# A new order of pieces in a two-block transformer kernel, with its weight splits written into it

## The chip, the cores and the metric

One core of a Trainium2 chip runs the whole program. The metric is the device time of one execution in microseconds. The kernel before took 2286.56 us (median of three runs, 2283.53 to 2306.3).

## The reference

Activations are 256 tokens of 1024 features in float32. The first block has two layers, each of: SwiGLU (width 2816), a mixer, cross attention onto 256 memory tokens, SwiGLU. The mixer of layer 0 is differential attention beside stick-breaking attention; that of layer 1 is latent attention (MLA, 16 heads). The second block has two layers, each of three mixers on one projection, an output projection with layer norm, and a SwiGLU with layer norm:

```python
o_gla = _gla_mixer(...)        # gated linear attention, 4 heads
o_rwkv = _rwkv7_mixer(...)     # delta-rule recurrence, 4 heads
o_nsa = _nsa_mixer(...)        # 8 heads: compressed, selected, window attention
mix = jnp.concatenate([o_gla, o_rwkv, o_nsa], axis=-1) @ w_out[l]
x = _layer_norm(DEEPNORM_ALPHA * x + mix, ln1_w[l], ln1_b[l])
```

NSA's output is `gt[0]*o_cmp + gt[1]*o_slc + gt[2]*o_win` per head. With 256 tokens, the selection takes in every block, so the kernel computes the second and third parts as two causal attentions with keys and values of their own.

## The kernel before

**Stages.** Twelve stages run in the order f0, m0, c0, f1, f2, m1, c1, f3, b0, f4, b1, f5: `f` is a SwiGLU, `m0` and `m1` are the mixers of the first block, `c0` and `c1` its cross attentions, `b0` and `b1` the three mixers of the second block with output projection and layer norm. The activation `x` stays in SBUF as eight slices of 128 features by 256 tokens.

**Weights.** Every weight is read once, in units of up to 128x1024 values, by SyncE's queue into a ring of 6 buffers (`RING`). A float32 product is made of three reduced-precision ones, so each unit is split: ScalarE writes the rounded part (`w_hi`), VectorE the rest (`w_lo`), and TensorE multiplies hi by hi, hi by lo and lo by hi. There are 4 pairs of buffers for split units (`NU`). A split has to wait for its load and for TensorE to have used the unit that held the pair before. `act_splits` and `dve_splits` (lines 376 and 391) are called after every piece; each splits all units that the next piece needs, and further ones if a test (`can_split`) on the orders allows it.

**Pieces and orders.** A stage is a list of pieces, such as "the second half of the query projection" or "step 1 of attention unit 5". All five engines walk through the same list, and each does its own share of a piece, in order; semaphores keep them together where data pass. So a piece is short on one engine and long on another, and a piece in the wrong place makes an engine stand in front of a wait while later work is ready. In the `f` stages the list is written by loops. In the six others it is a string (`WEAVE`, line 40): every letter names a chain, and takes that chain's next piece (`woven`, line 1204). In `c0`, `p` is the query chain (projection half, sum of squares, projection half, norm, turns), `a` to `d` are four attention units of three steps (scores, turn, values), and `o` is the output projection and the eight updates of `x`. In `b0` and `b1`, `r` is the delta rule's main chain and `s` its second inner part, `g` and `h` gated linear attention, `l` and `n` the projections and the compressed part of NSA, `u` `v` `w` `a` `b` five lanes of its 16 attention units, and `m` the output projection and the layer norm.

**Fillers.** The letter `z` is a "warm" piece: TensorE alone does something there, the product of two identity matrices into a PSUM bank that is known to be idle (`pe_warm`, line 3092). One such float32 product is recorded as two matmuls of 128 columns. Where no bank is known to be idle, nothing is issued.

**Update of x.** `act_x`, `dve_x` and `pool_x` (lines 644 to 668) prepare the next stage's input for each slice: ScalarE rounds it, VectorE computes the rest, GpSimd adds up squares. A root mean square (`rs`) needs all eight squares; TensorE sums them over partitions.

**GLA.** Scores within a chunk are summed over seven levels (`ge`). Each level takes differences on GpSimd, exponentials on ScalarE, two multiplies on VectorE, eight matmuls into two banks, and a masked multiply of each bank on VectorE; from level 1 on GpSimd adds the two results onto the matrix `P` (lines 2783 to 2870).

**NSA.** Compressed attention writes `mix`; each of 16 attention units then adds its gated output onto `mix` (line 2202 on). The five lanes' score buffers lie over buffers of the compressed part.

## Time and profile before

| | |
|---|---|
| runs | 2283.53, 2286.56, 2306.3 us |
| span of the profiled execution | 2285.3 us (no other time of it is listed) |
| TensorE matmul busy | 2202.2 us, 96% |
| VectorE, ScalarE, GpSimd busy | 1526.7, 1104.3, 418.3 us (67%, 48%, 18%) |
| weight splits on VectorE | 571 instructions, 694.2 us |
| DMA | 310.32 MB, mean 136 GB/s |

A busy TensorE only says that matmuls were running, fillers too. "PEclk" is the granted clock of TensorE as a share of 2.4 GHz. L140 is the line of the one helper that issues all matmuls, L165, L171, L177, L182 and L192 those of VectorE's and GpSimd's operations, L154 and L191 those of ScalarE's; tiles have to be told by their names (`ps` PSUM, `consts` the identity, `ring`, `w_hi`, `w_lo` weights, `scratch` the stage buffers, `rows` the squares).

### The profile page before, as it was taken

Reading aid. Unit: us, or ns where it says so; the run is one execution under the profiler, and the core shown is the slowest. Engines: PE = TensorE matmul, PEld = TensorE weight load, DVE = VectorE, ACT = ScalarE, POOL = GpSimd, SP = SyncE. Lnnn points to the kernel's source line nnn. Section 1 sums busy time; section 2 is a strip of 40 time slices with the busy share of each in tenths; the row PEclk is TensorE's granted clock in tenths of the full one; section 3 lists DMA queues with packets and bytes.
Section 4 is the critical chain, followed back from the end, with each engine's and each line's share of the span. In section 5 each row is a group of like instructions: output and inputs, shape, how many; then the busy total and the mean of one; then the engine's idle time right before and its main releaser. Section 6 shows DMA issues by size and latency. Waiting matters only on the chain.

```text
span 2285.3 us, 36711 instructions
## 1 busy us (share of the span) xinstructions
PE 2202.2 (96%) x14388; PEld 1953.8 (85%) x14388; DVE 1526.7 (67%) x2709; ACT 1104.3 (48%) x1997; POOL 418.3 (18%) x379
## 2 busy tenths in 40 slices
PE   6999999999999999999999998999998999999997
PEld 5888888988888888999888987889887988788886
DVE  5976765587678667756876685456766586456765
ACT  4654454365456544535654522346555432345554
POOL 2521001122112100012220030101213123101223
PEclk9999999999999999999999999999999999999999
DMA  6545432254555443133544321114544320303552
GB/s 242 192 170 173 148 130 74 74 192 182 180 194 190 177 157 133 38 111 130 188 179 174 139 85 61 57 38 152 186 181 149 133 94 1 116 29 127 187 178 90
DMA packets 88444, 310.32 MB, mean 136 GB/s; under 512 B 9808, under 2 KB 11600, under 8 KB 87760
## 3 DMA queue, kind: packets, MB, share of 16 engines
q1 hardware_dynamic: 87984, 305.29, 37.5%
q8 instruction: 114, 1.87, 0.3%
q10 hardware_dynamic: 288, 2.69, 0.3%
q14 instruction: 58, 0.48, 0.1%
HBM read 306.89 MB, written 1.05 MB: 135 GB/s over the span
## 4 chain that ended last, share of the span: by engine, by line
PE 91%; DVE 4%; ACT 2%; DMA 1%; issue 1%; POOL 0%; SPq 0%; DVEq 0%; ACTq 0%; POOLq 0%
PE ps L140 89%; PE ps L145 2%; DVE scratch L165 2%; DMA ring<-in_w 1%; ACT w_hi L154 1%; DVE w_lo L165 1%; ACT scratch L154 0%; DVE x L165 0%; DVE scratch L192 0%; DVE stats L182 0%; POOL scratch L165 0%; ACT scratch L191 0%; DVE scratch L177 0%; DVE scratch L171 0%; SPq L207 0%
## 5 line engine op out<-in xcount | busy, mean ns | idle before, releaser
L165 DVE TENSOR_TENSOR w_lo<-ring,w_hi 128x1024 fp32r<-128x1024 f32 (+2 forms) x571 | 694.2, 1230 | 420.0 <-ACT w_hi L154 414.3
L140 PE MATMUL ps<-h,w_hi 128*128 128x512 f32 (+1 forms) x2784 | 872.2, 372 | 24.0 <-DVE h L177 19.1
L154 ACT ACTIVATE w_hi<-ring 128x1024 fp32r<-128x1024 f32 (+2 forms) x571 | 581.5, 1032 | 487.0 <-PE ps L140 485.4
L140 PE MATMUL ps<-h,w_lo 128*128 128x256 f32 x2448 | 688.0, 281 | 0.0
L140 PEld LDWEIGHTS ps<-h,w_hi 128*128 128x128 f32 x2784 | 504.2, 190 | 123.3 <-issue 21.4
L140 PEld LDWEIGHTS ps<-h,w_lo 128*128 128x128 f32 x2448 | 465.0, 190 | 0.0
L140 PE MATMUL ps<-f,w_hi 128*128 128x512 f32 (+1 forms) x1444 | 419.2, 356 | 3.2 <-DVE f L165 3.2
L140 PE MATMUL ps<-f,w_lo 128*128 128x256 f32 x1184 | 331.9, 280 | 0.0
L165 POOL TENSOR_TENSOR f<-f_work,f 128x256 fp32r<-128x256 f32 x132 | 187.7, 1422 | 596.2 <-ACT f L154 596.1
L140 PEld LDWEIGHTS ps<-f,w_hi 128*128 128x128 f32 x1444 | 254.4, 189 | 46.1 <-DVE w_lo L165 3.6
L140 PE MATMUL ps<-scratch 128*128 128x128 f32 (+9 forms) x1952 | 256.3, 300 | 8.7 <-DVE scratch L192 2.5
L140 PE MATMUL ps<-consts 128*128 128x128 f32 x1912 | 246.5, 280 | 0.0
L140 PEld LDWEIGHTS ps<-consts 128*128 128x128 f32 x1912 | 233.5, 195 | 10.3 <-issue 6.1
L140 PEld LDWEIGHTS ps<-scratch 128*128 128x128 f32 (+4 forms) x1952 | 210.4, 186 | 33.0 <-issue 10.7
L140 PEld LDWEIGHTS ps<-f,w_lo 128*128 128x128 f32 x1184 | 223.9, 189 | 0.1
L191 ACT ACTIVATE scratch<-ps 128x512 f32<-128x512 f32 (+9 forms) x203 | 98.5, 499 | 221.7 <-PE ps L140 171.8
L140 PE MATMUL ps<-w_hi,h 128*128 128x512 f32 (+2 forms) x528 | 161.2, 380 | 0.1
L165 POOL TENSOR_TENSOR rows<-x 128x256 f32<-128x256 f32 x64 | 40.7, 636 | 589.5 <-DVE x L165 583.1
L165 DVE TENSOR_TENSOR f_work<-f_work,ps 128x256 f32<-128x256 f32 x306 | 126.6, 415 | 3.6 <-ACT f_work L191 3.5
L165 POOL TENSOR_TENSOR scratch<-scratch 128x512 f32<-128x512 f32 (+1 forms) x69 | 87.9, 1276 | 201.1 <-DVE scratch L165 83.6
L165 DVE TENSOR_TENSOR f_work<-f_work 128x256 f32<-128x256 f32 x264 | 113.8, 431 | 8.6
L140 PEld LDWEIGHTS ps<-w_hi,h 128*128 128x128 f32 x528 | 98.8, 190 | 15.9 <-issue 1.2
(136 smaller groups left out, 2136.4 us busy)
## 6 DMA issues: line engine op xcount, KB each, us to landing
ring<-in_w SPq DMA_DIRECT2D x520, 512.0 KB, 3.3
ring<-in_w SPq DMA_DIRECT2D x48, 384.0 KB, 3.4
ring<-in_w SPq DMA_DIRECT2D x16, 396.0 KB, 4.8
stage_consts<-in_ctwo ACTq DMA_DIRECT2D x1, 1344.0 KB, 5.9
stage_consts<-in_cthree ACTq DMA_DIRECT2D x1, 1281.0 KB, 6.8
stage_consts<-in_cone SPq DMA_DIRECT2D x1, 1083.0 KB, 5.7
x<-in_x SPq DMA_DIRECT2D x4, 256.0 KB, 4.4
scratch<-in_m SPq DMA_DIRECT2D x1, 1024.0 KB, 6.7
```

The costliest lines, as they stand in the source:

```text
L140: return self.e.matmul(out, lhsT, rhs, start=start, stop=stop, skip_group_check=free)
L145: return self.e.transpose(out, x, self.K.ident[0:x.shape[0], 0:x.shape[0]])
L154: return self.e.activation(out, x, func, **k)
L165: return self.e.tensor_tensor(out, a, b, op)
L191: return self.e.activation(out, a, ACT.Copy)
```

## The change

- **Strings.** All six `WEAVE` strings are new. Fillers go from 1009 to 287 marks (b0 282 to 55, b1 284 to 71, c0 95 to 36, c1 86 to 36, m0 80 to 24, m1 182 to 65). Two new marks place weight splits: `.` is the next unit's split on ScalarE, `,` on VectorE (131 and 146 of them). In stages with such marks the automatic calls only split what the next piece needs; in the `f` stages they are as before. The other letters come as often as before, but for `b` (gone in the blocks), `u` to `a` and `m`.
- **`dve_x`** does the update of slice j before the rest of slice j-1 and not behind it.
- **GLA.** From level 1 on, VectorE copies each bank straight into `P` where the level's mask is set (`copy_predicated`), and GpSimd adds nothing. Some waits name other steps in turn.
- **NSA.** Attention units write into an accumulator of their own (`ao`); a new piece `nA`, once for each half of the tokens, adds it to `mix` on VectorE. There are 4 lanes for 5, the buffers lie elsewhere, and the keys are rotated in the order 1, 2, 0, 3.
- **Latent attention.** The two latent vectors get buffers of their own in place of those of the stage's input, and queries, outputs and the fifth lane move. TensorE turns the output in pieces of the new layout.

The strings with their marks, and the core of the rest:

```diff
@@ -37,27 +37,23 @@
 NORMED = ("f0", "m0", "c0", "f1", "f2", "m1", "c1", "f3")
+MARKS = {"z": "warm", ".": "split_hi", ",": "split_lo"}
 WEAVE = {
-    "b0": ("zzzzzzzzzrzzrrrrrgzgzgrhlzhzhzzzzrzzzhzzzzzzzrzzhrzzzhzgzzhzzzzzzzhzzzzzzzzhzzhzzzzzzzzzzrzzzzzz"
-           "zzzzhhrhzzzzzzzhzzzzzzlzhzzzzhzrrrzzhzrlhzhzzrrzszzzhzrzsrzzzhzzzsszhzzzzzszzszzzzznzzzzzzzzzzrz"
-           "rzzzzzzzzsrnznzrzzzzzzrznzzzzzzzznnnzzzzzzzzzznzzwzzzzzzzzzzzzzzzzzzzzzrzzzzzzzzzzzzzzzzvrsvrrnz"
-           "zzzzzzrzzrnrnzrzzzzzzzzzzzrwzzrurnrsunsuwvsrsbsusrvrrruzvbrvrarvrwbabuwurwaawrauramurzvzwbuabzbv"
-           "awzzbumabummzmzzzmmmmmmmzmmmmzzzzzzzzzzzmmzzmzmmmmmmzmzmzmzzmzzzzzzzzmzzzmzzzzzmmmmzzzz"),
-    "b1": ("zzzzzzzzzzrzrrgrzgrgrhgzzrrlhzzzzzzzzzzzzzzzzzzzzzhhzzzrzzzrzzhhzzhzzzzzzzzzzzzzzzzzzzzzzzzzzzzz"
-           "zzzzzzzzzzzzzrhhhzzrzzhzzhzzzzzzlzzzrzzrzzzzzzzzzzzrrhhzrshzzhzsrzzlsszhrhszzrhzrrhrzhsrhzzzzzzz"
-           "zzszrzzzzszrzzznrzszzzzzznzrsnrzzznzznzzzzzznrrrnwzzzzzzzzzzzzzzzzzzzzzzznzzzzzzzzzzruzzzzzzzzzz"
-           "zzzzzzzzzzzzzzzzzrsrwnzrznzszzszzrsrzzrrnzrrnrnrzurvrwwbuavrrvmrvzzrvzzzzazbubvwbauawwuaubwvauab"
-           "buvuwvazbuambummmzzzzmzmmmmmmzmzzzzmmmzmmmmmmmmzzzzmzzzmzzzzzmzmzzmzmzzzzmzzzzmzmzzzzmzzm"),
-    "c0": ("zzzzzzzzzpppzzzzpzzzzzzzzzzzzzzzzzzzzzzzzzzzzzzzzzzzzzzzzzzzpzpazcbacdbzacdbdozozzzozoozoozzozoo"
-           "zzzzzzozozzzzzzzzzzzozzzzzzzzz"),
-    "c1": ("zzzzzpppzzzpzzzzzzzzzzzzzzzzzzzzzzzzzzzzzzzzzzzzzzzzzzppazbdazbcdabcdcozzoozozozzooozozzzoozzzzz"
-           "zzzzzzzzzzzzzzzoozzzz"),
-    "m0": ("zzypzzzzzqqzzzzzqzzzzzzzzkzkqzzpzzzzzzzzzzzzzzzzkyzzzzzzykbakyqlycvaycvbaabcacbcaacctbsbatscaacc"
-           "tassactszczssotzystzztssyzzzootsttotstoozzozzzzzzzzozzoozozoozoozzzzzozoozzzzzz"),
-    "m1": ("zyzpzzzzzqqzqzkkqzyzqyzzkzqqzqkzzzqkzzzzzzzzzzzzzzzzzzzzzzzzzzzzzzzzkzzzzzzzzzzzzzzzzzzzzzzzzzzz"
-           "zzzzzzzzzzzzzkzzzzzzhzzzzzzzzzzzzzzzzzyzzzzzzzyzttzzttzzzzyztzzzzzzzzzttztzzzzzzzzzzzzzuzuzyuayu"
-           "zuucauducbadacbedacbedbacaebcodaceabcbedadebecdzaobedaeoozozzzozoozoooooozozzzzozozzzzzzzzzzzzzz"
-           "z"),
+    "b0": ("r,.,.r..,,r,,..r,.r.r,zzzzzzzzzrrrrhg,.,.gzzrrgzzzhh.h.zzzzzrrzh,,rrrhh,.gh,,hs,.hhsl,h.,s,.hh,h"
+           "rzzlrrh.hr.rhhrhs,s,,h.,rhlrszrnzzzrszzzznnrzzzrnzzzzznzzzzznzznwsuvarruwswruaruaavwsrvursruwsaw"
+           "ravwausrruwvnsrvvurwravzznranr.w.rvurnur.wvaru,mvrnrnma,wvam.m,mmmmzzzzm,.mmmmmm..,,..,mmmmmmmmm"
+           "mmmzzzzmmmmmmmmmm"),
+    "b1": ("zzzzzzzzzzzzzzzzzzr,.,.r,,..r.,.,r.,r.zzhr.g,,.r,r.g,.rrg.,,.,.,zzzhhhg..r,h,rlhhzrrrrh,,h,r,hrh"
+           "zzzzlhr,,h,sh,hszzlrhrrshhrshsrhrhsrhzzzrsnzzzzsrzzzzzzzzznnzzzzzzzzzznrnzzznzzznruvsruwsuawrsra"
+           "uwvwarawvrsurvrwsarvrnaswauurrvrwuaznrwn.ruu.ravrawunrm,varvnrwvr.n,.mwvu,avmm,mm.mmzzzzm,mmmm,m"
+           ",mm,mm....mmmmmmmmmzzzzmmmmmmmmmm"),
+    "c0": (".pppp..zzzzzzzzzzzzzzzzzzzzzzzzzzzzzzzzp,pzbcabdcabdc.ad.ozo,zzooo.,oo.o,oo.o,o,,o"),
+    "c1": ("pp.,ppzzzzzzzzzzzzzzzzzzzzzzzzzzzzzzzzp..pzbadbc,adbcadc.ozozzo,oo.,o,.o,ooo.,.o,oo"),
+    "m0": ("q..p,,q.,,.zby,,p.b,,b,,.k.q,,..tsk,,zzzzzzb,.,yky.sq,tkk,.qa.v..,,c.,lva.c,,ya..a,.y.a.,cca,a,y"
+           "b.c,ab.ccaasctsctazzsctascstctozzzzzzzzztsyttssyzzoo,tst,.o..,s,o..oo,zzzzo.o.o.o,ooo,ooo,,,o"),
+    "m1": ("yqp,..,q.q,.zzzzkqq,,..zzzzzzq.k.,q.,.k,q..,,,k,y,q.,yk,,,..zzzzzzzzzzzzzzzzzzzzzzzzzzzzzzzu.uu."
+           "zzk.,ku.,yh.uyzzzzzzzzzzzzztttacbedtttttuyebuca...dzzcecazzayzdybceadbuccabd,aebd,c,adbaaee,bdco"
+           "aeodabeoo,.oo,zzzzo.o..oo,ooo.,ooo.,o,"),
 }
@@ -196,6 +192,9 @@
         if self.name == "act":
             return self.act(out, a, ACT.Copy, scale=s)
         return self.ts(out, a, s, None, MUL)
+    def where(self, out, mask, x):
+        return COUNTED if self.e is None else self.e.copy_predicated(out, mask, x)
     def set(self, out, v):
+        self.ck = tuple(f[:, 10240 + 512 * i:10752 + 512 * i].rearrange("p (k t) -> p k t", k=2) for i in range(2))
         self.f_both = f[:, :].rearrange("p (k n) -> p k n", k=22)
         self.f_hi, self.f_lo = (self.f_both[:, :, 256 * i:256 * i + 256] for i in range(2))
         self.f_work = make("f_work", 3072)
         self.h = (self.h_hi, self.h_lo)
-        make("between", CR0 + 2048 - 18432)
+        make("before_cq", 2048)
...
+def dve_split(e, K):
+    u = K.pairs[e.next_split]
+    if u.pair >= NU:
+        e.wait_ge(*K.used(K.pairs[u.pair - NU]))
+    e.wait_ge(*K.loaded(u))
+    e.wait_ge(*K.at("split_hi", u.n))
+    e.tt(u.los, u.src, u.his.bitcast(F32), SUB).then_inc(*e.up("split_lo", u.n))
+    e.next_split += 1
+def act_splits(e, K, early):
     while e.next_split < len(K.pairs):
         u = K.pairs[e.next_split]
-        before = K.pairs[u.pair - NU] if u.pair >= NU else None
-        if u.piece > e.piece + 1 and not can_split(e, K, u, before):
...
@@ -654,6 +668,8 @@
 def dve_x(e, K, s, j, add=None):
+    if add and j < 8:
+        add()
     if j:
         x_wait(e, K, s, j - 1)
         n, k = AFTER[s], j - 1
@@ -661,8 +677,6 @@
         hi, lo, x = K.h_hi.bitcast(F32)[:, k, :], K.h_lo[:, k, :], K.x[:, k, :]
         ins = e.stt(lo, x, K.gain(n)[:, k:k + 1], hi, MUL, SUB) if n in NORMED else e.tt(lo, x, hi, SUB)
         ins.then_inc(*e.up("split_x", (n, k)))
-    if add and j < 8:
-        add()
-        self.qT = K.area(11264, 4096, h=16, t=256)
+        self.qT = K.area(0, 4096, h=16, t=256)
         self.kT = K.area(15360, 4096, h=16, t=256)
-        bufs = [(K.area(o, 384), K.area(o + 384, 384)) for o in (19456, 20224, 20992, 21760, 0)]
-        self.o = K.area(4096, 2048, t=2, n=D)
+        bufs = [(K.area(o, 384), K.area(o + 384, 384)) for o in (19456, 20224, 20992, 21760, 14336)]
+        self.o = self.q.rearrange("p t (g n) -> p t g n", g=8)[:, :, :, 0:128]
...
         self.qT = K.area(G, 1024, k=4, t=256)
-        self.k2 = K.area(G + 1024, 512, t=2, g=2, e=2, d=64)
-        self.KS = K.area(G + 1536, 512, g=2, t=256)
-        self.kT = [K.area(G + 2048 + 512 * i, 512, g=2, t=256) for i in range(3)]
-        self.vT = K.area(G + 3584, 512, g=2, t=256)
-        self.ra, self.rb = K.area(G + 4096, 1024), K.area(G + 5120, 1024)
-        self.PT = K.area(G + 4096, 2048, i=16, t=128)
-        self.XC = [K.area(G + 6144 + 480 * i, 480, j=16, g=2, c=15) for i in range(2)]
-        self.hid, self.hu = K.area(G + 7104, 256), K.area(G + 7360, 256)[0:94]
-        self.cT = K.area(G + 7360, 192, k=2, n=96)
+        self.kT = [K.area(o, 512, g=2, t=256) for o in (G + 2048, G + 1024, G + 1536)]
+        self.vT = K.area(G + 2560, 512, g=2, t=256)
+        self.KS = K.area(G + 3072, 512, g=2, t=256)
+        self.XC = [K.area(G + 3584 + 480 * i, 480, j=16, g=2, c=15) for i in range(2)]
+        self.PT = K.area(G + 2048, 2048, i=16, t=128)
+        self.k2 = K.area(G + 4608, 512, t=2, g=2, e=2, d=64)
+        self.ra, self.rb = K.area(G + 5120, 1024), K.area(G + 6144, 1024)
+        self.hid, self.hu = K.area(G + 7168, 256), K.area(G + 7424, 256)[0:94]
+        self.cT = K.area(G + 7424, 192, k=2, n=96)
         self.kc = K.area(G + 7680, 32)
         self.vc = K.area(G + 7712, 128, g=2, d=64)
+        self.ao = K.area(GN, 1024, t=2, n=512)
         self.S = K.area(G + 7840, 240, t=2, h=8, c=15)
         self.gate = K.area(G + 8080, 48, t=2, n=24)
         self.gate4 = self.gate.rearrange("p t (h a) -> p t h a", h=8)
         self.kk = self.kv[:, :, 0:768].rearrange("p t (a g d) -> p t a g d", a=6, g=2)
-        bufs = [(K.area(o, 384), K.area(o + 384, 384)) for o in (G + 1024, G + 6144, G + 8128, G + 4096, G + 4864)]
+        bufs = [(K.area(o, 384), K.area(o + 384, 384)) for o in (G + 8128, G + 4608, G + 5376, G + 6144)]
@@ -2080,10 +2110,9 @@
                 "g": some("gp", 3) + [("gl", 0)], "h": [("ga", 0), ("gt", 0), ("gd", 0), ("gx", 0), ("gx", 1)]
                 + [("ge", (n, s)) for n, s in level_order()] + some("gO", 3),
                 "l": some("np", 3),
-                "n": ([("nq", 0)] + some("nqT", 2) + some("nk", 4)
-                      + some("nc", 3) + some("nS", 3)),
-                **lanes("A", 16, 5, "uvwab"),
-                "m": some("ms", 2) + [("out", (0, 0)), ("out", (1, 0))] + [("mT", 2), ("mT", 3)]
+                "n": [("nq", 0)] + some("nqT", 2) + [("nk", a) for a in self.nk] + some("nc", 3) + some("nS", 3),
+                **lanes("A", 16, 4, "uvwa"),
+                "m": some("ms", 2) + [("out", (0, 0)), ("out", (1, 0)), ("nA", 0), ("nA", 1), ("mT", 2), ("mT", 3)]
                 + ln_pieces(self.stage, [[("out", (j // 4, 1))] if j % 4 == 0 else [] for j in range(8)])}
...
@@ -2208,20 +2237,26 @@
         dve_delta(e, K, T, what, i)
     elif what[0] == "g":
         dve_gla(e, K, T, what, i)
+    elif what == "nA":
+        e.wait_ge(*K.at("evicted", (s, "ncmp", i)))
+        for u in range(1, 16, 2):
+            e.wait_ge(*K.at("evicted", ((s, "n"), u, "o")))
+        e.tt(T.mix[:, i, :], T.mix[:, i, :], T.ao[:, i, :], ADD).then_inc(*e.up("added", (s, "n", i)))
     elif what[0] == "n":
         dve_nsa(e, K, T, what, i)
     elif what == "A":
         u = i[0]
         h, a = u // 2, 1 + u % 2
-        o = lambda q: T.mix[:, q, 64 * h:64 * h + 64]
+        o = lambda q: T.ao[:, q, 64 * h:64 * h + 64]
         if i[1] == 2:
-            if u == 0:
-                e.wait_ge(*K.at("evicted", (s, "ncmp", 1)))
             if a == 2:
                 e.wait_ge(*K.at("evicted", ((s, "n"), u - 1, "o")))
+            else:
+                e.wait_ge(*K.at("turned", ((s, "nqT"), 1)))
         dve_attn(e, K, T.A_, *i,
                  lambda r: e.then(e.tt(r.unsqueeze(2), r.unsqueeze(2), T.gate4[:, :, h, a:a + 1], MUL)),
-                 lambda q, ps, rs: e.stt(o(q), ps, rs, o(q), MUL, ADD))
+                 (lambda q, ps, rs: e.ts(o(q), ps, rs, None, MUL)) if a == 1 else
+                 (lambda q, ps, rs: e.stt(o(q), ps, rs, o(q), MUL, ADD)))
     elif what == "ms":
...
-                m = T.P[p] if n == 0 else (E, xq)[p].rearrange("p k t -> p (k t)").rearrange("p (h t) -> p h t", h=4)
+                m = T.halves[2 * HALVES[n]]
                 e.wait_ge(*K.at("scores", (s, n, p)))
-                e.tt(m, b, bc(T.halves[2 * HALVES[n]], 4), MUL).then_inc(*e.up("evicted", (s, "ge", n, p)))
+                if n:
+                    e.wait_ge(*K.at("evicted", (s, "ge", n - 1, p)))
+                ins = e.where(T.P[p], bc(m.bitcast(I32), 4), b) if n else e.tt(T.P[p], b, bc(m, 4), MUL)
+                ins.then_inc(*e.up("evicted", (s, "ge", n, p)))
...
-            for p in range(2):
-                if n:
-                    m = (T.gE[n % 3], T.XQ[n % 2])[p].rearrange("p k t -> p (k t)").rearrange("p (h t) -> p h t", h=4)
-                    e.wait_ge(*K.at("evicted", (s, "ge", n, p)))
-                    e.then(e.tt(T.P[p], T.P[p], m, ADD), "added", (s, n, p))
...
+    act_splits(e, K, True)
     for name, T, order in stages(K):
+        early = ("split_hi", 0) not in order
         for what, i in order:
-            if what == "warm":
-                continue
-            e.piece += 1
-            ACTE[T.kind](e, K, T, what, i)
-            act_splits(e, K)
+            if what == "split_hi":
+                act_split(e, K)
+            elif what not in MARKS.values():
+                e.piece += 1
```

## Rows read from the trace of the kernel before

**Rows 1.** Page, the chain of waits that ended last, shares by engine

```profile
PE 91%; DVE 4%; ACT 2%; DMA 1%; issue 1%; POOL 0%; SPq 0%; DVEq 0%; ACTq 0%; POOLq 0%
```

**Rows 2.** Windows by stage: m0 with c0, f1, m1 with c1, b0, b1

```profile
core 0: us, PE busy (x) PEld busy (x) DVE busy (x) ACT busy (x) POOL busy (x), PEclk, DMA share, GB/s
209.00:455.00 246.00, 239.44 (x1571) 214.35 (x1572) 154.41 (x297) 109.50 (x193) 22.25 (x29) 0.99 0.31 108
455.00:636.00 181.00, 181.00 (x1049) 158.12 (x1048) 134.63 (x216) 101.06 (x171) 39.88 (x35) 1.00 0.51 183
818.00:1062.00 244.00, 235.62 (x1641) 217.25 (x1639) 165.21 (x341) 109.62 (x216) 23.64 (x31) 0.99 0.27 96
1244.00:1567.00 323.00, 307.37 (x2392) 275.45 (x2392) 194.01 (x396) 123.48 (x255) 44.91 (x35) 0.98 0.22 79
1758.00:2087.00 329.00, 313.21 (x2385) 279.13 (x2384) 202.21 (x416) 139.19 (x279) 53.48 (x43) 0.97 0.20 73
```

**Rows 3.** Page, groups of instructions: the fillers (count, busy us, mean ns, idle before)

```profile
L140 PE MATMUL ps<-consts 128*128 128x128 f32 x1912 | 246.5, 280 | 0.0
```

**Rows 4.** Timeline of TensorE in c0 (start us, us, engine line, operation, count)

```profile
405.75 10.66 PE L140 MATMUL ps<-consts 128*128 128x128 f32 x94
416.25 1.04 PE L145 MATMUL ps<-consts,scratch 128*128 128x128 f32 x8
```

**Rows 5.** Timeline of VectorE in c0: two weight splits, the norm's last multiply

```profile
407.04 2.36 DVE L165 TENSOR_TENSOR w_lo<-ring,w_hi 128x1024 fp32r<-128x1024 f32 x2 [0.33 <-ACT w_hi L154]
...
414.25 1.22 DVE L165 TENSOR_TENSOR scratch<-scratch,stage_consts 128x1024 f32<-128x1024 f32 x1
```

**Rows 6.** Timeline of TensorE in m1: fillers beside the query norm

```profile
885.85 7.31 PE L140 MATMUL ps<-consts 128*128 128x128 f32 x64
```

**Rows 7.** Timeline of VectorE in m1: first and last of that norm's operations

```profile
886.36 3.35 DVE L182 TENSOR_REDUCE stats<-scratch 128x32 f32<-128x3072 f32 x1 [1.37 <-ACT scratch L154]
...
901.68 1.22 DVE L165 TENSOR_TENSOR scratch<-scratch 128x1024 f32<-128x1024 f32 x1
```

**Rows 8.** Timeline of ScalarE in m0: two splits that waited for TensorE

```profile
219.37 1.06 ACT L154 ACTIVATE w_hi<-ring 128x1024 fp32r<-128x1024 f32 x1 [2.87 <-PE ps L140]
222.09 1.06 ACT L154 ACTIVATE w_hi<-ring 128x1024 fp32r<-128x1024 f32 x1 [1.66 <-PE ps L140]
```

**Rows 9.** Windows in b0, columns as in rows 2

```profile
1400.00:1465.00 65.00, 57.85 (x474) 48.65 (x473) 31.18 (x78) 18.86 (x43) 5.82 (x3) 0.97 0.27 102
1465.00:1525.00 60.00, 59.21 (x437) 49.65 (x437) 31.27 (x113) 26.95 (x88) 5.64 (x3) 0.97 0.01 1
```

**Rows 10.** Timeline of TensorE at the end of b0

```profile
1559.81 5.41 PE L140 MATMUL ps<-consts 128*128 128x128 f32 x47
```

**Rows 11.** Timeline of ScalarE at the end of b0, first of eight pairs

```profile
1561.32 0.60 ACT L154 ACTIVATE h<-x,consts 128x256 fp32r<-128x256 f32 x1 [0.49 <-DVE x L165]
1561.82 0.58 ACT L154 ACTIVATE x<-x,consts 128x256 f32<-128x256 f32 x1
```

**Rows 12.** Timeline of VectorE at the end of c0

```profile
443.61 3.13 DVE L165 TENSOR_TENSOR w_lo<-ring,w_hi 128x1024 fp32r<-128x1024 f32 x2 [0.90 <-ACT w_hi L154]
...
447.06 0.41 DVE L165 TENSOR_TENSOR x<-x,ps 128x256 f32<-128x256 f32 x1
...
448.52 0.41 DVE L165 TENSOR_TENSOR x<-x,ps 128x256 f32<-128x256 f32 x1
```

**Rows 13.** Timeline of GpSimd at the end of c0: squares of two slices

```profile
447.62 0.61 POOL L165 TENSOR_TENSOR rows<-x 128x256 f32<-128x256 f32 x1 [1.95 <-DVE x L165]
...
449.28 0.61 POOL L165 TENSOR_TENSOR rows<-x 128x256 f32<-128x256 f32 x1
```

**Rows 14.** Timeline of TensorE at the head of m0 (one of two)

```profile
211.60 1.84 PE L140 MATMUL ps<-consts,rows 128*128 128x1 f32 x8 [4.50 <-issue]
```

**Rows 15.** Window at the head of m0, columns as in rows 2

```profile
209.50:217.50 8.00, 5.90 (x23) 5.54 (x24) 6.73 (x25) 5.70 (x13) 0.61 (x1) 0.57 0.37 122
```

**Rows 16.** Groups of GpSimd in b0 (count, busy us, mean ns, idle before)

```profile
L165 POOL TENSOR_TENSOR scratch<-scratch 128x512 f32<-128x512 f32 x20 | 27.3, 1367 | 80.7 <-DVE scratch L165 43.1 <-ACT scratch L191 36.4 <-PE ps L140 0.3
```

**Rows 17.** Groups of VectorE in b0: additions in SBUF, masked multiplies from PSUM

```profile
L165 DVE TENSOR_TENSOR scratch<-scratch 128x512 f32<-128x512 f32 x33 | 23.1, 730 | 17.8 <-ACT scratch L191 10.3 <-ACT scratch L154 7.2
...
L165 DVE TENSOR_TENSOR scratch<-ps,stage_consts 128x512 f32<-128x512 f32 x14 | 9.0, 683 | 0.5 <-PE ps L140 0.5
```

More of the change, by code:

```diff
@@ L1081, with __init__ @@
 class Attn:
-    def __init__(self, K, name, lanes, q, k, v, dv, mask, bufs, stats, ready, values, col=None):
+    def __init__(self, K, name, lanes, q, k, v, dv, mask, bufs, stats, ready, values, col=None, free=None):
         self.name, self.lanes, self.q, self.k, self.v, self.dv, self.mask = name, lanes, q, k, v, dv, mask
@@ L1086, in __init__ @@
         self.col = col or (lambda u: 0)
+        self.free = free or (lambda u: [])
         self.w0 = 256 if mask is None else 128
@@ L1143, in act_attn @@
             e.wait_ge(*K.at("turned", (A.name, u - A.lanes)))
+        for w in A.free(u):
+            e.wait_ge(*w)
         for q in range(2):
@@ L1204, in woven @@
 def woven(stage, chains):
-    chains["z"] = [("warm", i) for i in range(WEAVE.get(stage, "").count("z"))]
+    for mark, piece in MARKS.items():
+        chains[mark] = [(piece, i) for i in range(WEAVE.get(stage, "").count(mark))]
     its = {k: iter(c) for k, c in chains.items()}
@@ L2835, in dve_gla @@
             y = T.gmix
+            for n in range(3):
+                e.wait_ge(*K.at("summed", ((s, "np", n), 1)))
             dve_head_ln(e, K, (s, "g"), T.gE[1], y)
```

131 lines of the change are left out of this document (77 added, 54 removed).

## The prediction

> **What bounds the kernel now.** I read the chain of waits first: nine tenths of it are matmuls, so the time is TensorE's own stream [rows 1]. The windows by stage then part that stream in two. A feed-forward stage (row 455 to 636) has TensorE busy for all of its 181 us, and the change leaves its pieces alone. The woven stages (m0 with c0, m1 with c1, b0, b1) fill 246 + 244 + 323 + 329 = 1142 us; TensorE is recorded idle in 6.6 + 8.4 + 15.6 + 15.8 = 46 us of them, and VectorE is busy in only 60 to 68% [rows 2]. So they look full, but they aren't: 1912 matmuls of the whole kernel are identity times identity, which is 956 fillers of two [rows 3] out of 1009 marks `z`. The row of 94 such matmuls starts at 405.75 and the next real work at 416.25: 10.50 us for 47 fillers, 0.223 us each [rows 4]. 956 x 0.223 = 213 us of filler plus 46 us of recorded idle is 259 us in which TensorE does nothing of use. That is the pool the change can draw on.
>
> A filler is worth nothing to remove if the data behind it is late anyway. In c0 VectorE's last multiply of the query norm ends at 414.25 + 1.22 = 415.47, and the turn that needs it starts at 416.25 [rows 4, 5]. The run of 47 was cut to within 0.8 us of the data. Thus the question for each run of fillers is: does the new order make the data come sooner, or give TensorE other work?
>
> **Where the gain is.** Within c0, the two weight splits at 407.04 (2.36 us) stand in VectorE's queue ahead of that norm [rows 5]. Placed earlier, they take 2.36 us off the chain. The new string has 32 fillers there, 15 fewer, 3.3 us. In m1 VectorE works on one piece (the norm and rotation of the queries) from 886.36 until 902.9 without a split. TensorE runs dry soon after and turns 32 fillers in one row of 7.31 us, and more behind it [rows 6, 7]. A unit of weights feeds TensorE for 2.72 us (the distance of two splits that waited for it), and four split units fit in the buffers: 10.9 us [rows 8]. Had all four been split before that piece of 16.5 us, about 5.6 us would be left dry; the new string keeps 31 fillers there, 6.9 us, which fits. So placing splits by hand is a real mechanism: work in hand replaces filler. In the blocks the same is done with attention. Now 1400 to 1465 holds short dependent steps and many fillers, and 1465 to 1525 the attention units, with VectorE at 31 us in each stretch [rows 9]. The units start late because they add onto the compressed result and share buffers with it; given an accumulator of their own and buffers elsewhere they can fill the first stretch.
>
> **The sum,** against the span 2285.3 us. No execution time of this profiled run is listed beside it; the median of three runs is 2286.6, the span 1.3 below, so I give span and time as one.
> - Fillers: the strings have 287 marks left. All are taken as issued: 956 - 287 = 669 go, x 0.223 = **-149**.
> - Stage ends of b0 and b1: 70 of these marks stand behind the last attention work (86 before, 16 after), 15.6 us. There the layer norm's own chain sets the pace: 23 fillers stand in one row from 1559.81 while ScalarE makes two passes, 0.50 us from start to start, for each of eight slices from 1561.32 [rows 10, 11]. None of that changes. The filler becomes bare idle: **+15.6**.
> - Ends of m0, c0, m1, c1: 110 marks (124 to 14), 24.5 us. Two splits (3.13 us at 443.61) delay the last slices of x [rows 12] and can go ahead, about 3 us for each of the four ends, 12 in all. The new order inside `dve_x` lets VectorE add slice j before it waits for ScalarE's rounding of slice j-1, where a step now takes 1.46 us (447.06 to 448.52). But GpSimd's squares step at 447.62 and 449.28, 1.66 us apart and back to back, and the root mean square waits for them before TensorE's last k [rows 13]: I cost this edit at nothing, GpSimd covers it; without that cover four slices at about 0.5 us, 2 us an end, would show. Stays: **+12.5**.
> - Heads of m0 and m1: TensorE waits 4.50 us for a sum of squares put ahead of the projection (two such waits, the other in m1), though the projection's first slices are ready. The new strings of both stages put half of it (`q`) ahead of `p`: **-9** [rows 14].
> - Short runs of one or two marks: 173 before, 36 after, 137 x 0.223 = 31 us. They bridged round trips between engines, some of which stay. I leave two thirds as waits (nothing and all are the ends, 0 and 31): **+20**.
> - Clock: behind the wait of 4.50 us TensorE's granted clock is 0.57 over 8 us, 3.4 us of full clock lost [rows 15]. Two such waits go (-7), six stage ends become bare idle of 3 us or more (+2.5 each, an estimate between half of that loss and all of it, since shorter gaps may cost less): **+8**.
> - GLA masks: per block 12 masked multiplies become predicated copies straight into P and 12 GpSimd additions of 1.37 us go (16 us of GpSimd, of 20 such operations). The trace has no predicated copy. The lower end is a masked multiply of the same sizes, 0.68 us, the upper end two passes, 1.37 us (as 1024 elements, 1.18 at 407.04); no row lets it cost less. I take 0.68, same operands: 0. Upper end for 24: 17 us of VectorE, half of it on the chain of levels, +8. The additions' exit leaves a shorter wait for the last level, which I count in the fillers [rows 5, 16, 17].
> - The separate accumulator costs two additions of 0.73 us per block in front of the turn, **+3** [rows 17]. Four attention lanes for five cost nothing as long as other pieces stand between the units; if lanes alone set the pace, a fifth of the 60 us stretch, 12 us a block. TensorE is busy for 59.2 of those 60 us now, so I take 0 [rows 9]. The waits added elsewhere (for buffers laid over one another, in GLA, NSA and the latent stage) all name steps that stand earlier in the strings; what queues behind `nq`'s wait for the last GLA level is VectorE's delta work. I cost them at 0, upper end 10 us, since the nearest waits of this kind are under 3 us. No DMA is added and the order of loads moves only with the units.
>
> Sum: -149 + 15.6 + 12.5 - 9 + 20 + 8 + 3 = -99: **2186 us**, 0.957 of the time now.
>
> **The rivals.**
> 1. *The order works as its marks say.* Short waits and ends close as well: -149 - 9 + 8 = -150 and some of the 28 us of the ends stay: 2120 to 2150. For it: in the kernel before the marks hit the data within 0.8 us in c0. Against: the layer norm chain is untouched. Chance 0.15, 2140.
> 2. *Dependent chains hold in the blocks.* Of 180 + 160 fillers removed between head and end of b0 and b1 (76 us) only a third goes, since the delta steps (multiply, evict, multiply) take turns between three engines whatever stands between them: 51 us less, with the upper copy price 2245, without it 2237. For it: one unit of attention also needs VectorE in order, behind whatever delta step waits. Against: VectorE has over a third of its time free in both blocks [rows 2]. Chance 0.20.
> 3. *Filler turns into waiting.* The ends of the chains don't move at all, 2270 to 2290. Only the 0.8 us of c0 speak for it, and the splits in the wrong place speak against. Chance 0.08.
> 4. *Slower: bare idle takes the clock.* Fillers go, the data isn't sooner, and the work after each gap runs at 1.2 GHz. Place: the 19 runs of ten marks or more that go (25 before, 6 after), like the one at 885.85. Each would be followed by a stretch such as the one after the 4.50 us wait, which lost 3.4 us; at 1.7 to 3.4 us each 32 to 65 us, time 2318 to 2350, middle 2335. It decides if the chains shorten by less than what the clock takes, some 50 us of the 149. Against it: the longest gaps keep 31 and 32 fillers. Chance 0.07.
>
> The Trainium skill, page "TensorE: Matmul & The Clock Gate", section Part 1, says that the idle state of the array is the throttled one and that only activity releases it, so that gaps should be kept out. By that rule the fillers earned their place and this change, which takes out 669, is on the wrong side; the time by it would be that of rival 4. The trace agrees as far as it goes: 0.57 behind the wait, 1.00 in the feed-forward row [rows 2, 15].
>
> **How the numbers follow.** My own case has 0.50, 2150 to 2225. The predicted time is its sum. The range 2115 to 2255 takes in rivals 1 and 2 for the most part, and leaves out some 0.2. A run of this kernel tells a change of about 1% from none (2264 to 2308 is the same). Faster: 0.50 + 0.15 + 0.20 = 0.85; same 0.08; slower 0.07.
>
> **What would show it.** Right: about 574 identity matmuls; woven windows of some 1040 us in all; feed-forward rows unchanged at 100% and 181 us; m0's and m1's first wait gone; attention rows between the delta rows of a block; GpSimd's 128x512 group down from 20 to 8 a block. Wrong: TensorE's recorded idle in the woven windows well above 46 + 40 us (rival 2 or 3), or the granted clock of b0 or b1 under 0.9 (rival 4). The predicated copy's mean against 0.68 us tells the price I had to bound.

## The result and the profile after

The changed kernel takes 2159.8 us (four runs, 2158.47 to 2168.95) against 2289.96 us for the kernel before (four runs beside it). The ratio is 0.9433, 95% interval 0.9403 to 0.9462: 130 us less. The forecast was 2186 us, 26 us too slow, inside its range. The profiled execution is the slowest of the four, 2168.95 us with a span of 2167.2 us.

From the page of the changed kernel, the shares of the chain of waits by engine (before: [rows 1]) and the group of VectorE's splits:

```profile
PE 84%; DVE 9%; ACT 3%; issue 2%; DMA 1%; POOL 1%; SPq 0%; ACTq 0%; DVEq 0%; POOLq 0%
...
L161 DVE TENSOR_TENSOR w_lo<-ring,w_hi 128x1024 fp32r<-128x1024 f32 (+2 forms) x571 | 697.0, 1231 | 309.8 <-ACT w_hi L150 308.6
```

The filler group after, for [rows 3], and the new predicated copies, for [rows 17] (groups of the whole kernel):

```profile
L136 PE MATMUL ps<-consts 128*128 128x128 f32 x516 | 67.7, 283 | 0.0
...
L197 DVE COPY_PREDICATED scratch<-stage_consts,ps 128x512 f32<-128x512 int32 x24 | 16.0, 724 | 0.0
```

516 matmuls are 258 fillers; 29 of the 287 marks found no free bank. 698 fillers are gone, 155.7 us at 0.223. The changed kernel issues the same work otherwise: 12992 - 516 = 12476 matmuls, and 14388 - 1912 = 12476 before. Now the four woven stretches, from the last wide matmul of the feed-forward stage ahead to the first of the one behind. Before:

```profile
198.69:448.70 250.01, 241.56 (x1603) 216.86 (x1601) 158.38 (x300) 112.88 (x196) 19.67 (x26) 0.99 0.33 113
813.24:1056.93 243.69, 235.31 (x1650) 217.55 (x1649) 166.05 (x342) 109.53 (x215) 19.69 (x26) 0.99 0.28 99
1236.62:1564.98 328.36, 312.73 (x2443) 280.99 (x2441) 196.82 (x399) 125.22 (x256) 44.91 (x35) 0.98 0.23 82
1743.91:2083.58 339.67, 320.49 (x2443) 286.24 (x2441) 207.92 (x419) 141.00 (x279) 55.11 (x46) 0.96 0.22 80
```

and after, columns as in [rows 2]:

```profile
198.16:418.05 219.89, 214.86 (x1385) 190.23 (x1384) 155.51 (x298) 111.06 (x196) 23.38 (x25) 1.00 0.37 121
783.36:992.71 209.35, 202.03 (x1330) 179.22 (x1329) 162.22 (x337) 105.18 (x212) 22.78 (x24) 1.00 0.33 109
1177.04:1480.78 303.74, 285.38 (x1991) 248.27 (x1989) 195.59 (x396) 126.26 (x254) 29.35 (x23) 0.89 0.26 87
1659.27:1963.54 304.27, 281.65 (x2036) 246.86 (x2035) 205.60 (x416) 135.38 (x273) 38.05 (x34) 0.93 0.26 87
```

The sum goes from 1161.7 to 1037.2 us, 124.5 less. TensorE's idle time is about the same (51.6 and 53.3 us), though 156 us of filler are gone: the places of these fillers are filled with work, or closed. Of the gain 29.5 us are given back as clock: the busy time without fillers was 1110.1 - 213.2 = 896.9 us and is 983.9 - 57.5 = 926.4 us for the same matmuls, with the granted clock of b0 at 0.89 for 0.98 and of b1 at 0.93 for 0.96. The rest of the span, the feed-forward stages, is 6.4 us longer. -124.5 + 6.4 = -118.1, the difference of the spans.

### The profile page after: what moved, and what is told of

Same layout as the page of the kernel before. It is cut to its first block, busy times and chain, and to the rows that moved or that the text cites. A ratio compares the mean times of both kernels' runs of the same rounds, so it can differ in the third digit from the quotient of the medians.

```text
span 2167.2 us, 33860 instructions
## 1 busy us (share of the span) xinstructions
PE 2078.1 (96%) x12992; PEld 1819.2 (84%) x12992; DVE 1533.3 (71%) x2713; ACT 1102.1 (51%) x1997; POOL 404.1 (19%) x355
## 4 chain that ended last, share of the span: by engine, by line
PE 84%; DVE 9%; ACT 3%; issue 2%; DMA 1%; POOL 1%; SPq 0%; ACTq 0%; DVEq 0%; POOLq 0%
PE ps L136 82%; DVE scratch L161 3%; PE ps L141 3%; DVE w_lo L161 2%; ACT scratch L150 1%; DMA ring<-in_w 1%; DVE x L161 1%; DVE scratch L167 1%; POOL rows L161 1%; DVE scratch L173 1%; DVE stats L178 1%; ACT w_hi L150 1%; DVE scratch L188 0%; ACT L155 0%; DVE h L173 0%
## 5 line engine op out<-in xcount | busy, mean ns | idle before, releaser
L136 PE MATMUL ps<-h,w_hi 128*128 128x512 f32 (+1 forms) x2784 | 881.6, 375 | 35.4 <-DVE h L173 21.3
L150 ACT ACTIVATE w_hi<-ring 128x1024 fp32r<-128x1024 f32 (+2 forms) x571 | 582.7, 1032 | 422.5 <-PE ps L136 422.1
L136 PEld LDWEIGHTS ps<-h,w_hi 128*128 128x128 f32 x2784 | 511.6, 193 | 139.1 <-issue 29.5
L136 PEld LDWEIGHTS ps<-scratch 128*128 128x128 f32 (+4 forms) x1952 | 218.9, 195 | 31.0 <-issue 13.9
L187 ACT ACTIVATE scratch<-ps 128x512 f32<-128x512 f32 (+8 forms) x203 | 98.0, 503 | 217.2 <-PE ps L136 153.4
L161 POOL TENSOR_TENSOR rows<-x 128x256 f32<-128x256 f32 x64 | 52.9, 827 | 515.3 <-DVE x L161 508.9
L136 PE MATMUL ps<-w_hi,h 128*128 128x512 f32 (+2 forms) x448 | 134.6, 374 | 4.1 <-DVE w_lo L161 3.9
L150 ACT ACTIVATE scratch<-ps,stats 128x256 f32<-128x256 f32 (+2 forms) x140 | 61.4, 448 | 108.1 <-PE ps L136 56.5
L187 ACT ACTIVATE f_work<-ps 128x256 f32<-128x256 f32 x306 | 111.3, 366 | 1.3 <-PE ps L136 1.3
L141 PE MATMUL ps<-consts,scratch 128*128 128x128 f32 (+3 forms) x544 | 83.0, 289 | 15.9 <-DVE scratch L161 11.1
L136 PEld LDWEIGHTS ps<-w_hi,h 128*128 128x128 f32 x448 | 82.8, 188 | 17.7 <-DVE w_lo L161 4.9
```

The source lines that it names most:

```text
L136: return self.e.matmul(out, lhsT, rhs, start=start, stop=stop, skip_group_check=free)
L141: return self.e.transpose(out, x, self.K.ident[0:x.shape[0], 0:x.shape[0]])
L150: return self.e.activation(out, x, func, **k)
L161: return self.e.tensor_tensor(out, a, b, op)
L187: return self.e.activation(out, a, ACT.Copy)
```

## The experiments

The question was which part carries the gain. In every table below "idle" is the length of the four stretches less TensorE's busy time, and "rest busy" is the busy time less the fillers at 0.223 us, which shows the clock, since these are the same matmuls in every kernel. Time and ratio are medians of several runs; idle, stretches and waits are those of the one profiled run.

**1. Old strings in the mixer stages.** The strings of m0, c0, m1, c1 of before in the changed kernel:

```diff
-    "m0": ("q..p,,q.,,.zby,,p.b,,b,,.k.q,,..tsk,,zzzz...
+    "m0": ("zzypzzzzzqqzzzzzqzzzzzzzzkzkqzzpzzzzzzzzz...
```

> The changed kernel with the strings of m0, c0, m1 and c1 taken back to the ones before (no split marks there, so these four stages split early again); code, buffers and the strings of b0 and b1 stay. Theory (the strings carry the gain: fewer fillers and an earlier end of the stage): the two windows of the mixer stages were 250.0 and 243.7 us and are 219.9 and 209.4, so 64 us come back and the time is 2215 to 2232 us, with about 620 to 700 identity matmuls more than the 516. Rival (VectorE's addition ahead of its split and the new latent buffers carry it): under 2180 us.

Measured: 2217.9 us, ratio 0.9668 (0.9613 to 0.9723); the two stretches 250.4 and 242.4 us, as before. 58 us of the 130 are in these four strings with their marks, as the theory had it (with 538 identity matmuls more, somewhat fewer than expected). The blocks, with strings and code untouched, took 293.3 and 304.0 us here: b0 is 10 us shorter than in the changed kernel at a clock of 0.93 for 0.89. The same instructions cost 10 us more or less by where the clock falls.

**2. Old strings in the blocks,** fitted to four lanes. They have no marks, so these two stages split early again.

```diff
-    "b0": ("r,.,.r..,,r,,..r,.r.r,zzzzzzzzzrrrrhg,.,.g...
+    "b0": ("zzzzzzzzzrzzrrrrrgzgzgrhlzhzhzzzzrzzzhzzzz...
```

> The changed kernel with the strings of b0 and b1 taken back, fitted to four attention lanes for five (each attention piece keeps its place in the order, its letter is that of the lane which now holds it) and with the two new pieces put behind the last attention piece. Theory (strings): the windows were 328.4 and 339.7 and are 303.7 and 304.3, so 60 us come back, 2210 to 2230 us. Rival (the code of the blocks carries it: GpSimd's 12 additions a block gone, attention no longer behind the shared accumulator): under 2185 us, with as many fillers as before.

Measured: 2248.7 us, ratio 0.9799 (0.9749 to 0.9849). 89 us come back, more than the 60 expected: the blocks are 336.2 and 360.8 us, 29 us longer than in the kernel before. The fitted old order with the new code is worse than the old order with the old code. So the code of the blocks (lanes, accumulator, masks) doesn't carry the gain by itself. What the fitting to four lanes costs and what the code is worth isn't parted here. The 58 and 89 us add up to 147, more than the 130 of the whole change, so the two shares can't be read as parts of a sum.

**3. The order without its split marks.** Every `.` and `,` out, splits by the automatic rule:

```diff
-    "c0": (".pppp..zzzz...zp,pzbcabdcabdc.ad.ozo,zzooo.,oo.o,oo.o,o,,o"),
+    "c0": ("ppppzzzz...zppzbcabdcabdcadozozzooooooooooo"),
```

> The changed kernel with every split mark taken out of the six strings, so that each engine splits a weight as soon as its buffer is free, as before the change; the order of the pieces and the fillers stay. Theory of the prediction (early splits cost about 3 us at an end of a stage and little else): 2165 to 2180 us. Rival A (the placing is worth more, since an early split stands in front of evictions that TensorE waits for): over 2185 us, with more TensorE idle behind VectorE and ScalarE rows in the blocks. Rival B (no worth): 2155 to 2164 us.

Measured: 2289.8 us, ratio 0.9985 (0.9953 to 1.0017). The whole gain is gone, though pieces, fillers and code are those of the changed kernel. Rival A holds, and by 100 us more than its bound. The new order with a quarter of the fillers, but with early splits, is no faster than the old kernel. The profiled run is the fastest of the ten (2275.95 us), its span 107 us over that of the changed kernel: its stretches are 1142.9 us with 143.7 us idle, 90 more, and rest busy is 941.6 for 926.4, 15 us of clock. One such wait is in the first quarter of b0. VectorE in that run (start us, us, operation, count, idle before):

```profile
1290.15 1.37 DVE L200 TENSOR_TENSOR_SCAN scratch<-consts,scratch 128x128 f32<-128x128 f32 x4
1291.55 2.36 DVE L158 TENSOR_TENSOR w_lo<-ring,w_hi 128x1024 fp32r<-128x1024 f32 x2
1295.36 2.97 DVE L158 TENSOR_TENSOR w_lo<-ring,w_hi 128x1024 fp32r<-128x1024 f32 x2 [1.45 <-ACT w_hi L147]
1298.25 1.53 DVE L158 TENSOR_TENSOR scratch<-scratch 128x512 f32<-128x512 f32 x1
1299.82 1.29 DVE L164 TENSOR_SCALAR scratch<-scratch,stage_consts 128x256 f32<-128x256 f32 x2
```

and TensorE in the same run:

```profile
1301.26 2.05 PE L133 MATMUL ps<-scratch,stage_consts 128*128 128x512 f32 x2 [7.16 <-DVE scratch L164]
```

TensorE waits 7.16 us for two small operations, those of 1298.25 and 1299.82, and ahead of them in VectorE's queue stand four splits and a wait for ScalarE, 1291.55 to 1298.25, 6.7 us. The first two splits are needed four pieces on and stand at the same place in the changed kernel. The other two, 4.3 us with the wait for ScalarE, are needed fifteen pieces on, and the marks put them nine pieces later (counted over the two programs). The same place in the changed kernel, VectorE and then TensorE, which doesn't wait:

```profile
1234.57 3.50 DVE L161 TENSOR_TENSOR w_lo<-ring,w_hi 128x1024 fp32r<-128x1024 f32 x3
1237.98 0.69 DVE L161 TENSOR_TENSOR scratch<-scratch 128x512 f32<-128x512 f32 x1
1238.70 0.62 DVE L167 TENSOR_SCALAR scratch<-scratch,stage_consts 128x256 f32<-128x256 f32 x2
...
1240.79 1.02 PE L136 MATMUL ps<-scratch,stage_consts 128*128 128x512 f32 x2
```

The splits are not all of it: the two operations themselves took 2.86 us for 1.34, with GpSimd at work beside them in the run without marks (6.27 us from 1294.43) and not yet in the changed kernel (from 1240.97). The Trainium skill, page "TensorE: Matmul & The Clock Gate", section "Architectural detail: the array is 16× 32×32, not 1× 128×128", calls the queues of ScalarE and VectorE strictly first in, first out. The rows agree: the operation at 1298.25 starts as the split ahead of it ends.

**4. No fillers in the kernel before.** One edit, every `z` out.

```diff
-    "c0": ("zzzzzzzzzpppzzzzpzzzz...zpzpazcbacdbzacdbdozozzzozoozoozzozoo...
+    "c0": ("ppppppacbacdbacdbdooooooooooooo"),
```

> The kernel before without any of its 1009 filler marks (956 fillers issued, 213 us of identity matmuls); nothing else is changed. Theory 1, the prediction's (most fillers stand in the way, the waits behind them are small): 2080 to 2160 us, for the filler time goes and at most 20 to 60 us of it comes back. Theory 2, formed on the run without split marks (its order had 258 fillers and still took 2290 us, with 144 us of TensorE idle in the four windows where the changed kernel has 53): the early splits make TensorE wait, the fillers of before lay over these waits, and without them busy time turns into waiting one for one: 2270 to 2310 us, idle in the windows over 180 us, VectorE rows named as what it waits for.

Measured: 2300.5 us, ratio 1.0055 (1.0027 to 1.0083). Theory 2 holds. 213 us of filler go, idle rises from 51.6 to 199.3 us (+148), and the clock takes the rest: rest busy 966.4 for 896.9 (+70), granted clock 0.93, 0.89, 0.90, 0.86 in the four stretches. -213.2 + 147.7 + 69.5 = +4.0, the 3.9 us between the sums of the stretches; the feed-forward stages add 7. Behind the query norm of m1, where the kernel before had its row of 32 fillers [rows 6, 7], the profile now shows

```profile
903.07 0.80 PE L129 MATMUL ps<-w_hi,h 128*128 128x512 f32 x1 [13.77 <-DVE scratch L181]
```

The fillers of before were thus, taken together, not in the way. They lay over waits that its order had, and held the clock.

**5. Splits later by rule.** The marks put a split later than the automatic rule does, never earlier. Counted over the two programs, of ScalarE's 37 splits in b0 10 stand where the rule has them and the others later, 6.3 pieces in the mean over all and up to 40. The traces agree: of the 172 splits that VectorE takes in the four stretches, 115 have more of its other instructions ahead of them than in the run without marks, 57 as many, none fewer. So I moved the rule itself, with no marks:

```diff
-    return (before is None or before.piece <= e.piece) and ...
+    return (before is None or before.piece <= e.piece - e.slack) and ...
+        e.slack = 3 if name in WEAVE else 0
```

> The changed kernel without split marks (as in the run of 2290 us), with one change to the rule by which a split is taken early in the six woven stages: not as soon as the piece that last read its buffer has been issued, but three pieces later. No place is written by hand. Theory (the cost of the automatic place is that ScalarE and VectorE stand at a split until TensorE has come through the piece just issued, with the evictions behind it): the waits of the w_hi rows for TensorE shrink and most of the 130 us come back, 2165 to 2215 us. Rival (the marks are worth what they are because each stands at its own chosen place): 2250 to 2290 us, no better than the run without marks.

Measured: 2397.5 us, ratio 1.0458 (1.0416 to 1.0500). My theory of a uniform delay fell, and the rival was too mild. The waits of TensorE (whole kernel: us in total, times, longest):

```profile
PE ps L133 <- DVE w_lo L158: 116.2, 31, 12.3
PE ps L133 <- DVE h L170: 25.3, 3, 18.9
PE ps L133 <- DVE scratch L158: 18.4, 5, 7.8
```

Now it waits for the splits themselves. One piece of delay, to see whether there is a point between:

```diff
+        e.slack = 1 if name in WEAVE else 0
```

> The changed kernel without split marks, with the automatic rule moved by one piece (a split may be taken one piece after the last reader of its buffer was issued; at once gave 2290 us, three pieces later 2397 us). Theory (both ends cost, early splits hold the evictions and late ones hold the matrices, and only places chosen one by one avoid both): between or above the two, 2270 to 2350 us, with TensorE waiting for w_lo rows more than the 1 us of the automatic rule and less than the 116 us at three. Rival (one piece of delay is a good rule by itself): under 2230 us.

Measured: 2317.6 us, ratio 1.0110 (1.0082 to 1.0137), as the theory had it. The series, with the same order, fillers and matmuls in each kernel (time is the median; the profiled run of the first row lies 14 us under its median):

| splits | time | idle | TensorE waits for `w_lo` | for other data of the stages | ScalarE waits at `w_hi` for TensorE |
|---|---|---|---|---|---|
| at once | 2289.8 | 143.7 | 0.9 | 120 | 491.3 |
| one piece later | 2317.6 | 160.7 | 40.8 | 99 | 461.6 |
| three pieces later | 2397.5 | 215.0 | 116.2 | 73 | 426.2 |
| where the marks put them | 2159.8 | 53.3 | 7.7 | 27 | 422.1 |

(Last three columns: the waits view, whole kernel; "other" is the sum of the rows for `scratch`, `rows`, `m_lo` and `cq_lo`.) The last column is the theory's own quantity, and it falls as foretold: a split taken later waits less. But a delay for all splits trades one wait of TensorE for the other and loses on balance. A mark chooses per split, and keeps both low: in b0, 15 of ScalarE's 37 splits stand earlier than in the program that delays all by three pieces, and 21 later.

**6. Both halves of a simple repair on the old order:** no fillers, and splits three pieces later, in the kernel before.

```diff
-    "c0": ("zzzzzzzzzpppzzzzpzzzz...
+    "c0": ("ppppppacbacdbacdbdooooooooooooo"),
+        e.slack = 3 if name in WEAVE else 0
```

> The kernel before with two edits: no fillers, and splits in the woven stages three pieces later than automatic; the order of the pieces, the five lanes, the masks and the buffers are those of before. Theory (fillers and early splits together are the loss): 2120 to 2200 us, at least half of the 130 us that the change gave. Rival (the new order of the pieces is needed too, since the old one was laid out with its waits): 2230 to 2290 us, near the one without fillers.

Measured: 2489.3 us, ratio 1.0861 (1.0818 to 1.0903), outside both forecasts. TensorE waits 170.1 us for `w_lo` alone. The loss of 199 us is more than those of its two halves added up (10 us in experiment 4, 108 between the first and third row of the table): idle rises from 51.6 to 337.0 us and rest busy from 896.9 to 1014.3, so the clock takes 117 us where the two losses come together. It is no test of the piece order by itself. Whether the old order with splits placed well would be as fast was not tried; that stays open.

**7. The masks alone,** put into the kernel before:

```diff
-                e.tt(m, b, bc(T.halves[2 * HALVES[n]], 4), MUL)
+                ins = e.where(T.P[p], bc(m.bitcast(I32), 4), b) if n else ...
-                    e.then(e.tt(T.P[p], T.P[p], m, ADD), "added", (s, n, p))
```

> The kernel before with the GLA mask part of the change alone: levels 1 to 6 copied into the sum under their mask by VectorE (24 rows), GpSimd's 24 additions gone. Prediction's theory (VectorE's rows cost the same, GpSimd's additions were beside other work): within 4 us of before, and the 128x512 rows of GpSimd 8 a block for 20. Rival (GpSimd's additions held up the next level): 10 us or more faster.

Measured: 2286.6 us, ratio 0.9983 (0.9961 to 1.0005). No difference that can be told, as predicted. In b0 of that run GpSimd's group is down from the 20 of [rows 16]:

```profile
L165 POOL TENSOR_TENSOR scratch<-scratch 128x512 f32<-128x512 f32 x8 | 9.3, 1163 | 61.8 <-ACT scratch L191 36.4 <-DVE scratch L165 25.1 <-PE ps L140 0.3
L201 DVE COPY_PREDICATED scratch<-stage_consts,ps 128x512 f32<-128x512 int32 x12 | 7.9, 723 | 0.5 <-PE ps L140 0.5
```

**8. VectorE's old order of addition and split** in the changed kernel:

```diff
-    if add and j < 8:
-        add()
     if j:
         x_wait(e, K, s, j - 1)
...
+    if add and j < 8:
+        add()
```

> The changed kernel with VectorE's addition of a slice put back behind the split of the slice before (the order before the change), all else kept. Prediction's theory (costed at nothing, since GpSimd's squares cover it): within 5 us of the changed kernel, 2155 to 2165 us. Rival (the addition ahead frees TensorE's norm sums at the ends of stages): over 2170 us.

Measured: 2168.9 us (2167.37 to 2173.5), ratio 0.9461 (0.9440 to 0.9481): 9 us over the changed kernel's median, between the two expectations. The intervals of the two ratios overlap, but its trace has the same sign in the mixer stages, which the edit touches: stretches of 221.4 and 212.5 us for 219.9 and 209.4, and the gate and up matmuls of f1 and f3 130.3 and 130.9 us for 127.0 and 129.9. That is 8.9 us, with waits for `w_lo` of 13.7 us for 7.7. The spans of the two profiled runs, though, are the same (2166.4 and 2167.2 us), since b0, whose code the edit leaves alone, is 8.6 us shorter here at a clock of 0.92 for 0.89. So the edit is perhaps worth some 9 us, which these runs don't settle; I had costed it at nothing.

**9. The fillers that are left.** All `z` out of the changed kernel:

```diff
-    "c0": (".pppp..zzzz...zp,pzbcabdcabdc.ad.ozo,zzooo...
+    "c0": (".pppp..p,pbcabdcabdc.ad.oo,ooo...
```

> The changed kernel without any of its 287 filler marks (258 fillers issued, 516 matmuls of 67.7 us). Theory 1 (a filler is time in the way at the places where they still stand): up to 58 us less, 2102 to 2145 us. Theory 2 (what is left of them fills idle time that stays, so their going only turns busy into waiting): 2150 to 2170 us, clock unchanged. Theory 3 (they hold the granted clock up): the granted clock of the woven windows falls below the 1.00 of the mixer stages and 0.89 and 0.93 of the blocks, and the time is over 2175 us.

Measured: 2187.1 us, ratio 0.9533 (0.9481 to 0.9584), 27 us slower than with them. Idle 105.3 us for 53.3: 52 of the 57.5 us of filler turn into waiting. Rest busy 944.6 for 926.4, 18 us of clock. (That makes 10 us between the two profiled runs. The one is the fastest of its four, the other the slowest, so the rest of the 27 us lies between the runs.) Theory 3 holds with theory 2 behind it: what is left of the fillers stands for the most part on true waits and earns its place by the clock.

**10. More fillers.** 121 marks ahead of the 26 pieces that still wait 0.6 us or more:

```diff
-    "b0": ("r,.,.r..,,r,,..r,.r.r,zzzzzzzzzrrrrhg,.,.gzzrrg...
+    "b0": ("zzzzzr,.,.r..,,r,,..r,.r.r,zzzzzzzzzrrrrhg,.,.zzzzzzzgzzrrzzzzzzzzg...
```

> The changed kernel with 121 fillers more, each group ahead of one of the 26 pieces in which TensorE still waits 0.6 us or longer in the profile of the changed kernel, as many as fill four fifths of that wait; the other strings and marks stay. Theory (the clock is held by work on the array, and a filler ahead of a true wait is free): the time falls by 5 to 20 us, to 2140 to 2155 us, with the granted clock of b0 and b1 over 0.93. Rival A (the half-clock stretches come from the many small attention rows and not from the waits): 2155 to 2165 us, clock as before. Rival B (a filler costs its 0.22 us there too): up to 27 us slower, 2175 to 2187 us.

Measured: 2158.4 us (2156.34 to 2160.91), ratio 0.9412 (0.9392 to 0.9432), against 0.9433 (0.9403 to 0.9462): the fastest of all, but the same as the changed kernel by these intervals. The time is rival A's, the clock the theory's. Of the 121, 106 found a free bank. The two blocks:

```profile
1181.60:1469.90 288.30, 274.83 (x2077) 241.31 (x2075) 194.77 (x396) 125.82 (x254) 29.37 (x23) 0.96 0.28 91
1650.76:1955.50 304.74, 287.87 (x2111) 253.07 (x2109) 199.83 (x416) 135.37 (x273) 37.08 (x34) 0.94 0.26 87
```

The clock of b0 is up to 0.96 and rest busy down to 903.2 us, idle down to 40.2. This profile is of a run of 2160.91 us and that of the changed kernel of one of 2168.95, 9.2 us above its median where this one is 2.5 above: about half of the 12.6 us between their stretches is thus the spread between runs. And 55 more, behind every third piece of the attention stretch of b0 and b1:

```diff
-    ...znwsuvarruwswruaruaavwsrvursruwsaw...
+    ...znwsuzvarzruwzswrzuarzuaazvwszrvuz...
```

> The one with the 121 fillers ahead of waits, and 55 more, one behind every third piece of the attention stretch of b0 and b1, where TensorE shows no wait but ran at half clock for up to 34 us on end. Theory (the array is too lightly used by these rows, and fillers among them keep it at full clock): the half-clock rows in the attention stretch are gone, 12 us of fillers against 20 to 25 us of clock, so 5 to 15 us faster than with the 121 alone. Rival (fillers there cost 0.22 us each and the clock falls all the same): 8 to 15 us slower than with the 121 alone.

Measured: 2168.4 us, ratio 0.9448 (0.9423 to 0.9473): 10 us slower than with the 121 alone, though the two intervals overlap a little. The rival holds by the median. 52 more fillers were issued, 11.6 us, of which 4.6 came out of idle (35.6 us for 40.2); the clock of the blocks is 0.95 and 0.95 for 0.96 and 0.94, rest busy 903.2 us as it was. A filler ahead of a wait costs little and can hold the clock. Among busy rows it costs its 0.22 us, and here it gave no clock back.

## Why the prediction was right, and where it was not

- **What bounds it, right.** The pool of 213 us of filler and 46 us of idle was where the gain came from. It was read in the main as time in the way; experiment 4 shows that it was waiting under another name. That was rival 3, to which I gave 0.08. It holds for the old program, in which removing fillers alone gives -213 + 148 + 70. Likewise rival 4's mechanism, bare idle that takes the clock, is real there: 70 us, more than its 32 to 65, though the whole loss against the median is 10 us. Neither decided, because the change also removes the waits.
- **The split marks, the step that failed.** I costed them at 3 us for each of four ends and took them for earlier splits ("placed earlier, they take 2.36 us off the chain"; "had all four been split before"). They are later splits, and with the new order kept, taking them away costs the whole 130 us (experiment 3). The row that showed it was in my hands: the split ahead of the norm in [rows 5] is this very effect, and I counted it in one place of c0 and in the ends. The same in all the other places of the six stages was left uncounted.
- **Fillers,** -149: measured -155.7 for 698 (the 29 marks without a free bank).
- **Ends and short runs,** +15.6, +12.5, +20: too large. Idle in the stretches is 53.3 us for 51.6 where I expected 48 more. At the end of b0 TensorE waits 3.15 us at once, where 15.6 us had been set for two ends. 6.4 us more show in the feed-forward stages, whose first matmuls wait for slices and splits.

```profile
1480.78 0.76 PE L136 MATMUL ps<-h,w_hi 128*128 128x512 f32 x1 [3.15 <-DVE h L161]
```

- **Heads of m0 and m1,** -9: right. The wait for `rows` in the changed kernel is 0.7 us in all, against two of 4.50 [rows 14].
- **Clock,** +8: measured +29.5 in the profiled run, the term most undersized. The granted clock of b0 stood at 0.89, under the 0.9 that I had named as the sign of rival 4, and the time was still not rival 4's: that sign doesn't tell the two apart. I looked for the loss behind waits [rows 15]; the clock also fell in b0 while TensorE had none:

```profile
1367.00:1377.00 10.00, 10.00 (x51) 8.51 (x49) 4.80 (x15) 3.28 (x14) 0.00 (x0) 0.50 0.01 2
1407.00:1417.00 10.00, 10.00 (x46) 8.89 (x45) 3.19 (x11) 2.77 (x9) 0.00 (x0) 0.50 0.01 2
1417.00:1427.00 10.00, 10.00 (x41) 7.45 (x40) 3.19 (x9) 3.30 (x9) 0.00 (x0) 0.50 0.01 2
```

- **Masks,** 0: right, 0.724 us a copy for 0.683, 24 x 0.04 = 1 us, and GpSimd's group in b0 down to 8 as forecast. **`dve_x`,** 0: perhaps 9 us, if GpSimd did not cover it (experiment 8). The accumulator's +3 and four lanes at 0 were not tested alone.

In sum: ends, short runs, heads and accumulator were set at +42 and gave +1.7 of idle and +6.4 in the feed-forward stages, 34 too high; the fillers gave 7 more; the clock took 21.5 more. That is 19 us below the forecast for the profiled run, and the median lies another 9 below that run. That the number came so close is in part luck: the missing worth of the marks stood in the sum under another name, since I had let the fillers' time go without asking what would take away the waits beneath.

The Trainium skill, page "TensorE: Matmul & The Clock Gate", section Part 1, holds that gaps bring the clock down and activity releases it. Experiments 4 and 9 agree (70 and 18 us of clock when waits are left bare); the three rows above show the low clock without a recorded gap.

## What to carry to other kernels

Price a filler by what lies beneath it: remove all of them once, and what comes back as idle is waiting that only other places for the work can remove. In an engine's queue, work that is ready early is not free: a split taken as soon as its buffer allows stands ahead of an eviction that TensorE needs, and the same split three pieces later leaves TensorE without weights. Look in the waits view at what the late engine was doing just before, and place such work one by one.
